# Copying the neighbourhood values for two token tiles at once: 16 copies a layer in place of 32, in a kernel of two mixer layers and one recurrent layer

## The reference, cut to what matters

```python
def neighbourhood_attention(q, k, v, rpb):
    b, s, h, d = q.shape
    rows = s // GRID_W                       # 512 // 64 = 8
    kh = min(NA_KH, rows)                    # 8
    n_cb = GRID_W // NA_KW                   # 64 // 16 = 4 groups of queries
    kb = 2 * NA_KW                           # 32 columns of keys
    ...
    cb_start = jnp.clip(jnp.arange(n_cb) * NA_KW - NA_KW // 2, 0, GRID_W - kb)
    ...
    qg = q.reshape(b, rows, n_cb, NA_KW, h, d)
    kg = k.reshape(b, rows, GRID_W, h, d)[:, row_idx][:, :, :, col_idx]
    vg = v.reshape(b, rows, GRID_W, h, d)[:, row_idx][:, :, :, col_idx]
    logits = jnp.einsum('brcqhd,brkcjhd->brcqhkj', qg, kg,
                        preferred_element_type=jnp.float32) * (d ** -0.5) + bias
    logits = jnp.where(valid[:, :, None, None, :], logits, NEG_INF)
    p = jax.nn.softmax(logits.reshape(logits.shape[:-2] + (kh * kb,)), axis=-1)
    ...
    out = jnp.einsum('brcqhkj,brkcjhd->brcqhd', p, vg)
```

## Time and profile before

| | |
|---|---|
| median of 3 runs | 2372.79 us (2370.24 to 2383.06) |
| profiled execution, its time | 2371.9 us |
| profiled execution, its span from first to last instruction | 2370.1 us |
| TensorE / VectorE / ScalarE / GpSimd busy | 98% / 68% / 48% / 1% of the span |
| mean granted clock of TensorE | 0.995 of full speed |

### The profile page before, as it was taken

The page is one execution under the profiler, slowest core; times in us unless marked ns, Lnnn a source line. Parts: engine busy times, 40 slices in busy tenths (PEclk is TensorE's granted clock), DMA queues, the critical chain, the costliest instruction groups (busy, mean ns, idle before and its releaser), DMA issues.

```text
span 2370.1 us, 40655 instructions
## 1 busy us (share of the span) xinstructions
PE 2318.9 (98%) x16692; PEld 1989.6 (84%) x16692; DVE 1618.8 (68%) x2547; ACT 1144.0 (48%) x1949; POOL 24.0 (1%) x20
## 2 busy tenths in 40 slices
PE   8999999989999999999999999999999999999998
PEld 6999998846789999989999887567899998779687
DVE  7957665558679577689577654686786686682564
ACT  4535444467445354545344445674453455343623
POOL 0000001000000000000000010000000000000000
PEclk9999999999999999999999999999999999999999
DMA  5323342200233334333334422003333333222001
GB/s 155 107 90 102 113 158 91 87 14 18 72 89 100 97 94 115 95 93 104 94 98 117 165 83 80 22 1 90 89 99 98 104 106 118 84 85 72 1 10 65
DMA packets 276649, 205.89 MB, mean 87 GB/s; under 512 B 10673, under 2 KB 263569, under 8 KB 275953
## 3 DMA queue, kind: packets, MB, share of 16 engines
q1 hardware_dynamic: 275632, 195.96, 27.9%
q0 software_dynamic: 832, 7.33, 0.8%
HBM read 199.06 MB, written 2.10 MB: 85 GB/s over the span
## 4 chain that ended last, share of the span: by engine, by line
PE 87%; DVE 6%; ACT 3%; DVEq 2%; issue 1%; DMA 0%; ACTq 0%; SPq 0%
PE bank L1082 23%; PE bank L1174 10%; PE bank L1176 10%; PE bank L1175 10%; PE bank L1151 6%; PE bank L1152 6%; PE bank L1153 6%; PE bank L1360 4%; PE bank L1391 2%; PE bank L1343 2%; PE bank L1454 2%; PE bank L1404 2%; PE bank L1699 1%; PE bank L1301 1%; DVE h_lo L2682 1%
## 5 line engine op out<-in xcount | busy, mean ns | idle before, releaser
L2533 DVE TENSOR_TENSOR w_lo<-raw,w_hi 128x2048 fp32r<-128x2048 f32 (+2 forms) x117 | 240.4, 2055 | 160.0 <-ACT w_hi L1886 159.8
L1886 ACT CAST w_hi<-raw 128x2048 fp32r<-128x2048 f32 (+2 forms) x118 | 202.3, 1715 | 182.3 <-PE bank L1153 90.2
L1151 PE MATMUL bank<-hid_hi,w_hi 128*128 128x512 f32 x704 | 274.7, 390 | 0.9 <-DVE xT L2774 0.9
L1152 PE MATMUL bank<-hid_lo,w_hi 128*128 128x512 f32 x704 | 274.3, 390 | 0.0
L1153 PE MATMUL bank<-hid_hi,w_lo 128*128 128x512 f32 x704 | 273.9, 389 | 0.0
L1174 PE MATMUL bank<-h_hi,w_hi 128*128 128x256 f32 x864 | 245.0, 284 | 2.0 <-DVE w_lo L2718 1.5
L1176 PE MATMUL bank<-h_hi,w_lo 128*128 128x256 f32 x864 | 244.5, 283 | 0.0
L1175 PE MATMUL bank<-h_lo,w_hi 128*128 128x256 f32 x864 | 244.5, 283 | 0.0
L2718 DVE TENSOR_TENSOR w_lo<-raw,w_hi 128x1024 fp32r<-128x1024 f32 x144 | 175.4, 1218 | 3.2 <-ACT w_hi L1958 3.2
L1174 PEld LDWEIGHTS bank<-h_hi,w_hi 128*128 128x128 f32 x864 | 165.7, 192 | 3.9 <-issue 1.6
L1175 PEld LDWEIGHTS bank<-h_lo,w_hi 128*128 128x128 f32 x864 | 165.7, 192 | 0.9
(11 more groups left out here) (501 smaller groups left out, 5459.5 us busy)
## 6 DMA issues: line engine op xcount, KB each, us to landing
raw<-in_ffn_w_up SPq DMA_DIRECT2D x88, 512.0 KB, 5.3
raw<-in_ffn_w_gate SPq DMA_DIRECT2D x87, 512.0 KB, 4.0
raw<-in_ffn_w_down SPq DMA_DIRECT2D x96, 384.0 KB, 3.7
raw<-in_w_in SPq DMA_DIRECT2D x60, 512.0 KB, 4.6
raw<-in_w_out SPq DMA_DIRECT2D x24, 512.0 KB, 4.5
raw<-in_ffn_w_down SPq DMA_DIRECT2D x16, 512.0 KB, 4.4
t_bias<-in_t_rel POOLq DMA_DIRECT2D x2, 1792.0 KB, 10.8
raw<-in_w_in SPq DMA_DIRECT2D x8, 416.0 KB, 3.8
```

The costliest lines, as they stand in the source:

```text
L1151: pe.matmul(to, hi(k), hid_hi[:, k, :], start=(k == 0), stop=False)
L1152: pe.matmul(to, hi(k), hid_lo[:, k, :], start=False, stop=False)
L1886: act.copy(w_hi[:, at, 0:n], raw[:, at, 0:n]).then_inc(hi_ready[at], 1)
L2533: dve.tensor_tensor(w_lo[:, at, 0:n], raw[:, at, 0:n], w_hi[:, at, 0:n].bitcast(F32), ALU.subtract)\
```

## The change: what it does

A copy now takes one grid row of each of two neighbouring tiles: 32 partitions by 2 by 256 values, so that 16 copies a layer move the same bytes as 32 did. For this, the two key tiles of a copy's destination must hold the two token tiles of its source. Key tile 0 thus holds token tiles 0 and 2, key tile 1 token tiles 1 and 3; `NA_TILE` gives the place of a token tile, and the keys in `qk_T` and the table `na_rel` take the same order. The copies are issued in the order of `NA_COPIES` (half, group): the first half's three groups 0 to 2 once tiles 0 and 1 are there, then groups 0 and 1 of the second half once tiles 2 and 3 are there, then the rest. `na_v_loaded` becomes one semaphore for each of the two tensors, and TensorE waits for the first ahead of pair 0 and for the second ahead of the first pair of group 2. The pairs run group by group: heads 0 and 1, then heads 2 and 3 of group 0, and so on, so that group 2 begins with pair 4. The semaphore `small_loaded` is dropped and its copies count on `const_loaded` (12 instead of 10, after the 2 of the start).

```diff
+NA_TILE = [t // 2 + t % 2 * 2 for t in range(T)]
+NA_KEY_ROWS = [2 * NA_TILE.index(n) + r for n in range(T) for r in range(P // GRID_W)]
+NA_COPIES = [(0, 0), (0, 1), (0, 2), (1, 0), (1, 1), (0, 3), (1, 2), (1, 3)]
+N_NA_COPIES = len(NA_COPIES) // 2 * (P // GRID_W)
...
-    na, mla = ([(m, i, (h, h + 1)) for h in (0, 2) for i in tiles] for m in ("na", "mla"))
+    na = [("na", i, (h, h + 1)) for i in tiles for h in (0, 2)]
+    mla = [("mla", i, (h, h + 1)) for h in (0, 2) for i in tiles]
...
-        na_v_loaded = sem("na_v_loaded")
+        na_v_loaded = [sem(f"na_v_loaded{n}") for n in range(NA_B // 2)]
...
-                for t in range(T):
-                    sp.wait_ge(proj_copied, at_layer(l, N_COPY, N_COPY - T + t + 1))
-                    for b, a in enumerate(NA_AT):
-                        for r in range(P // GRID_W):
-                            kt, to = divmod((t * (P // GRID_W) + r) * NA_W, P)
-                            sp.dma_start(na_v[b // 2][to:to + NA_W, b % 2 * len(NA_KT) + kt, :],
-                                         proj[r * GRID_W + a:r * GRID_W + a + NA_W, t, NA_V:NA_V + G]).then_inc(na_v_loaded, 16)
+                for half, b in NA_COPIES:
+                    sp.wait_ge(proj_copied, at_layer(l, N_COPY, N_COPY - T + 2 * half + 2))
+                    for r in range(P // GRID_W):
+                        to, a = half * HD + r * NA_W, r * GRID_W + NA_AT[b]
+                        sp.dma_start(na_v[b // 2][to:to + NA_W, b % 2 * len(NA_KT):(b % 2 + 1) * len(NA_KT), :],
+                                     proj[a:a + NA_W, 2 * half:2 * half + 2, NA_V:NA_V + G]).then_inc(na_v_loaded[b // 2], 16)
...
-                        if p == FIRST["na"]:
-                            pe.wait_ge(na_v_loaded, at_layer(l, 16 * S // NA_W * NA_B // 2, 16 * S // NA_W * NA_B // 2))
+                        if PAIRS[p][0] == "na" and PAIRS[p][1] % 2 == 0 and PAIRS[p][2][0] == 0:
+                            pe.wait_ge(na_v_loaded[PAIRS[p][1] // 2], at_layer(l, 16 * N_NA_COPIES, 16 * N_NA_COPIES))
...
-                        pe.wait_ge(small_loaded, 16 * 10)
+                        pe.wait_ge(const_loaded, 16 * 12)
...
+                        cut = slice(NA_TILE[t] * P, (NA_TILE[t] + 1) * P)
...
-    qr, qc, kr, kc = np.ix_(np.arange(NA_ROWS), np.arange(NA_KW), np.arange(NA_ROWS), np.arange(NA_W))
+    qr, qc, kr, kc = np.ix_(np.arange(NA_ROWS), np.arange(NA_KW), np.array(NA_KEY_ROWS), np.arange(NA_W))
```

More of the change, by code:

```diff
@@ L757, in unit_cut @@
             return slice(z * HD, (z + 1) * HD)
-        small_loaded = sem("small_loaded")
         in2_done = sem("in2_done")
@@ L1001, in _ @@
                     sp.wait_ge(x_ready, at_layer(DEPTH - 1, 4, 3))
[L1002 to L1007, removed]
+                    sp.dma_start(cols2[:, :], A["cols2"]).then_inc(const_loaded, 16)
+                    sp.dma_start(na_flat[:, 0:N_SMALL_CONST], A["small"]).then_inc(const_loaded, 16)
+                    sp.dma_start(small("ln_g"), A["rwkv_ln_g_2"][0].partition_broadcast(P)).then_inc(const_loaded, 16)
+                    sp.dma_start(small("ln_b"), A["rwkv_ln_b_2"][0].partition_broadcast(P)).then_inc(const_loaded, 16)
+                    sp.dma_start(small("lora_w")[0:RW_LORA], A["rwkv_w2_2"][0]).then_inc(const_loaded, 16)
+                    sp.dma_start(small("lora_w")[RW_LORA:2 * RW_LORA], A["rwkv_a2_2"][0]).then_inc(const_loaded, 16)
                     for name, w in (("w_a", "lru_w_a_2"), ("w_x", "lru_w_x_2")):
@@ L1010, in _ @@
                             sp.dma_start(small(name)[par * HD:(par + 1) * HD].rearrange("i (h j) -> i h j", h=2),
-                                         A[w][0, par::2].rearrange("h i j -> i h j")).then_inc(small_loaded, 16)
+                                         A[w][0, par::2].rearrange("h i j -> i h j")).then_inc(const_loaded, 16)
                 load_columns2(n, A["w_in_2"], pieces)
@@ L2498, in rwkv @@
                 split(DEPTH, PAN2_OUT + 1, PAN)
-            act.wait_ge(small_loaded, 16 * 10)
+            act.wait_ge(const_loaded, 16 * 12)
             project2()
@@ L3290, in forget_sums @@
                 dve.wait_ge(forget_ln, 1)
-                dve.wait_ge(small_loaded, 16 * 10)
+                dve.wait_ge(const_loaded, 16 * 12)
                 dve.scalar_tensor_tensor(forget, forget, 0.0, forget_abs, ALU.min, ALU.subtract)
```

## The result

| | before | after |
|---|---|---|
| median of 9 runs, us | 2371.12 (2369.52 to 2383.46) | 2355.08 (2349.35 to 2366.00) |
| profiled execution, us | 2371.9 | 2351.85 |
| mean granted clock of TensorE | 0.995 | 0.999 |

The ratio is 0.9937, with a 95% interval of 0.992 to 0.9955: faster by 0.6%, 16 us between the medians, where 19.2 was forecast. The runs of the changed kernel do not spread evenly: five of the nine lie between 2349.4 and 2355.1 (granted clock 0.998 to 1.000), four between 2363.2 and 2366.0 (0.991). The last experiments are about that gap.

What follows compares the result with a forecast made beforehand. TensorE was taken to bound the kernel (87% of the chain), stopped in two layers by SyncE's copy issue rate. Savings 9.66 + 9.87 = 19.5, less 0.3, took 2371.9 to 2352.7; plus 0.9 for the median, 2353.6 us, range 2349 to 2364.

Steps and rivals of the forecast that it cites:

- The wait and its cause: TensorE's stop before the first mixing matmuls, 7.37 and 7.58 us, comes from SyncE issuing 32 copies at 0.63 us each.
- p: Queue time to issue one new two-run copy on SyncE: taken as 0.75 us, between 0.63 and 0.91.
- L: Time from a new copy's issue start to its landing: taken as 2.0 us, between 1.9 and 3.1.
- Rival A: Copy issue costs by runs, 1.27 us each, so part of the stop stays: saves 7.1 to 13.9 us, 2362.3; chance 0.12.
- The saving: Per attention layer, TensorE's stop (7.37 and 7.58) plus slow clock (2.29 each): 9.66 + 9.87 = 19.5 us.
- The share of the clock: TensorE restarts at half clock after the stop: six pieces take 5.69 us instead of 3.40, costing 2.29 us a layer.
- So all of the pipeline moves forward by the gap: Behind the stop, ScalarE and VectorE keep TensorE's pace, so only 0.3 us is lost to tight steps: 19.2 us saved.
- The second wait: TensorE's wait for groups 2 and 3: copies land at 485.2 (487.8 at worst), asked for not before 490.0, so hidden.
- Pairs, keys, bias at 0: New pair order, key copy and host-built bias table in the attention cost 0; 1.7 us a layer if VectorE lacked time.
- Rival B: The stop goes but a later wait fixed in time, such as a load, gives the time back: 2372.8; chance 0.05.
- Rival C: Strided copies issue so slowly, up to 3.05 us each, that TensorE restarts 11.4 us later per layer: 2395.6; chance 0.04.

Runs made afterwards that it cites:

- The last experiments: Changed kernel with two short TensorE gaps in the recurrent layer filled by identity matmuls, 2354.06 and 2353.01 us; unchanged beside it, 2354.81 us.
- e2: Kernel after, but with pairs by heads and TensorE waiting for all 16 two-row copies ahead of pair 0: 2363.86 us.
- e3: Kernel before with its 32 single copies, those of groups 0 and 1 issued first, two semaphores, split wait and pairs group by group: 2351.68 us.
- e5: Kernel before with 48 identity matmuls put ahead of TensorE's wait for the copies: 2373.29 us.
- e7: e3 with its pairs back by heads, 32 copies: 2363.01 us.
- e4: Kernel before with its neighbourhood pairs by groups and nothing else changed: 2370.53 us, ratio 1.0008.
- e6: Changed kernel (16 copies) with its pairs back by heads: 2354.48 us.
- e8: e3 run again with nothing changed: 2363.89 us.
- e1: Changed kernel run again with nothing changed: 2353.66 us.
- e11: Changed kernel run a third time with nothing changed: 2354.81 us.

## Why the prediction was right

**The wait and its cause: right, shown.** That SyncE's issue rate set TensorE's restart, with the landing of the last copy, is shown by e2, whose chain runs through nine copies and a landing, and by e3, where the same 32 copies in 21 us hold up nothing.

**The price of a copy of two runs: right in direction, too dear in size.** I took p = 0.75 between 0.63 and 0.91; measured were 0.60 for an issue and about 0.64 from issue to issue. L was 2.0, as taken. The landing of groups 0 and 1 thus had 0.4 us to spare where 0.1 was forecast. Rival A (p = 1.27) is out. Its saving of 7.1 to 13.9 us was said to be half under 0.5% (11.9 us); by these numbers it is more than two thirds, which changes nothing here. The upper bound of p, 0.91, came from two shapes that issue in 0.43 and 0.71 us, and the difference was put down to the runs. The trace of before does not bear that out: copies of one line and one shape differ nearly as much, the loads of w_up at 0.58 and those of w_gate beside them:

```profile
L931 SPq DMA_DIRECT2D raw<-in_ffn_w_gate x87: 367/368/2182, 5.2 to 1940.3; - x87
```

What sets the time of one issue is open. The section "DMA Instruction — HWDGE (DVE, Sync)" of the Trainium skill's "Perfetto Trace Analysis", read as issue time in proportion to the runs, does not hold here: twice the runs cost 1%.

**The saving: mechanism right, size nearly.** Stop and slow clock were priced at 9.66 and 9.87 us; layer 2 gave 9.91, layer 1 8.24 with a star and, in e3 without one, 9.73. The share of the clock, 2.29, was measured by itself as 2.2 (e5). It is no fixed price of a stop: against e3 it is 1.6 to 2.6 us behind the shorter stops of e2 and e7.

**The step that was off** is "So all of the pipeline moves forward by the gap", with 0.3 us taken off for tight steps. The pipeline did move, but I treated the clock as 1.00 wherever the profile of before had it so. A short stretch at half clock, worth some 1.5 us, lies behind the copies in one of the two layers in seven of the eight profiles in which no stop is left (all but e3's), and others come and go in the third layer. In the lower group the difference is 17.5 us (means 2370.7 over 74 executions of the kernel before, 2353.2 over 15 of the changed one) where 19.2 was forecast, about one such stretch less. The rest of the way to the median of 2355.08 is the upper group, of which the prediction does not speak, though one of the three times of before was 2383.06. That the median still lies only 1.5 us from the forecast is in part luck: with five of nine executions in the upper group it would have been 2363 or more.

**The second wait: right.** It is hidden, and e7 shows what it costs without its cover: stops of 3.94 and 2.95 us on TensorE and 5.5 and 5.6 us more in the two layers than e3.

**Pairs, keys, bias at 0: right** (e4: +0.2 and +0.1 us). Rival B did not come: whatever was saved behind the copies is still saved at the output projection. Rival C did not come either, though single issues of 1.25 us occurred.

**What is not shown.** 12 of 86 executions of the kernel before lie in the upper group, 17 of 45 of the changed kernel and its equals. e4, with the length of the kernel before, had 4 of 12. Side by side on one chip e6 and e8 had 10 of 19 and the kernel before 3 of 26, which chance alone gives once in some 270 cases; yet e7 had none of 8 there, and on another chip e1, e3 and e11 had 3 of 17 beside 5 of 40. Whether the change makes the long stretch at half clock more frequent, by shifting the recurrent layer in time, is open. What ends the stretch is open as well. The new order of the copies and the split wait were not run one without the other. As an estimate from the earlier trace rows, with the old order the last copy of groups 0 and 1 is issue 28 of 32, so that a split wait alone would take 4 x 0.63 = 2.5 us off the stop of 7.4.

## What to carry to other kernels

When a consumer waits for many small copies of one queue, count the issues between the last input and the last copy that this consumer needs; the cure is to need fewer of them there, by order and by a semaphore for each part, and only then to have fewer of them. A stop of TensorE can have a second price in its clock behind it (here 1.6 to 2.6 us), which the profile lets one read off by comparing the same pieces further down. Three runs that lie as two and one may be two groups and not a spread: look at the granted clock of each, and for the stretch that makes the difference, before forecasting to 0.1%.

## What the runs showed of the hardware

The granted clock fell from 1.00 to 0.50 in the recurrent layer behind gaps of only 0.59 and 0.58 us, with TensorE busy 1.50 of the last 2.50 us and 9.40 of the 10 before, and stayed at 0.50 for 34 us in which TensorE was busy all the time (31.00 of the 31.00 us from 2279 in e8). The other three profiles of the upper group (e4, e6, e11) have the same fall behind the same gaps. Programs with these gaps kept the clock in most executions, and that the gaps are its cause is not shown. The two groups lie 11 to 12 us apart. The Trainium skill's page "TensorE: Matmul & The Clock Gate", section "HAM oscillation — how this bites in real kernels", tells of clocks lost to waits for transfers between bursts of matmuls; the stops in e2 and in the kernel before agree with it (3.7 and 7.4 us of waiting for copies, and half clock behind them). The long stretch came behind waits of 0.6 us for VectorE, no transfers, and stayed slow while TensorE was busy.

The length of a stop does not tell its price in clock. Behind 7.4 us of stop the first piece at full clock is 5.7 us behind the restart, behind e2's 3.7 us it is 6.0. In e7 a stop of 3.94 us cost 1.56 us of clock and one of 2.95 us cost 2.62.
